# Recurrence stage: the key and query products of 64-row heads, split into two groups around a level's second half

## The reference

```
def step(state, inp):
    r_t, w_t, k_t, v_t, a_t, b_t = inp
    sa = jnp.einsum('bhvk,bhk->bhv', state, a_t)
    state = (state * w_t[:, :, None, :]
             + sa[..., None] * b_t[:, :, None, :]
             + v_t[..., None] * k_t[:, :, None, :])
    y_t = jnp.einsum('bhvk,bhk->bhv', state, r_t)
    return state, y_t
```

## Time and profile before

| | |
|---|---|
| median of three runs | 3224.02 us |
| the profiled execution's own time | 3229.49 us |
| its span, first to last instruction | 3227.9 us |
| mean granted TensorE clock | 0.985 |
| recurrence stage, first L2508 to last gate | about 970 to 1256 us of the span |
| one turn | about 34.8 us |

### The profile page before, as it was taken

One profiled execution on the slowest core, in us unless ns is written; L12 is line 12 of the kernel. 1 busy time (PEld: TensorE's weight loads), 2 busy tenths in 40 slices (PEclk: granted clock), 3 DMA queues, 4 the chain that ended last, 5 costly groups with the idle time before them and its releaser, 6 DMA issues.

```text
span 3227.9 us, 65591 instructions
## 1 busy us (share of the span) xinstructions
PE 3116.5 (97%) x23394; PEld 2702.9 (84%) x23394; DVE 2223.6 (69%) x3345; ACT 1524.2 (47%) x2171; POOL 368.2 (11%) x546
## 2 busy tenths in 40 slices
PE   7999999999999999999999999999999999999998
PEld 6887877877888888888888888888888888888887
DVE  6658766588866775775767667776667757666675
ACT  5543444567546765443434334443444434344443
POOL 2001032100124541100000000100012000000002
PEclk9999999989999999999999999999999999999999
DMA  6555555456761113666666666677446666666664
GB/s 199 161 159 135 142 163 164 143 160 181 207 193 50 36 39 86 182 189 187 183 188 188 184 183 186 173 184 193 132 121 183 183 188 184 186 183 187 187 185 144
DMA packets 1001331, 524.53 MB, mean 163 GB/s; under 512 B 25734, under 2 KB 996380, under 8 KB 1000668
## 3 DMA queue, kind: packets, MB, share of 16 engines
q1 hardware_dynamic: 995756, 507.99, 56.2%
q0 software_dynamic: 4608, 13.31, 1.2%
q10 hardware_dynamic: 816, 1.11, 0.1%
HBM read 513.95 MB, written 8.39 MB: 162 GB/s over the span
## 4 chain that ended last, share of the span: by engine, by line
PE 86%; DVE 6%; ACT 3%; issue 3%; POOL 1%; DMA 0%; ACTq 0%; DVEq 0%; POOLq 0%; SPq 0%
PE proj L305 50%; PE proj L307 25%; DVE w_low L260 1%; PE side L2391 1%; ACT w_high L273 1%; DVE g L317 1%; PE side L2508 1%; DVE w_low L276 1%; ACT w_high L254 1%; PE side L2549 0%; PE side L2372 0%; PE side L549 0%; DVE g L2818 0%; DVE g L2822 0%; PE side L2423 0%
## 5 line engine op out<-in xcount | busy, mean ns | idle before, releaser
L305 PE MATMUL proj<-b_pair,w_high 128*128 128x512 f32 x3872 | 1377.0, 400 | 24.3 <-DVE b_pair L1128 9.9
L305 PE MATMUL proj<-a_pair,w_high 128*128 128x512 f32 x3664 | 1297.7, 399 | 36.9 <-DVE a_pair L1801 10.2
L276 DVE TENSOR_TENSOR w_low<-w_raw,w_high 128x1024 fp32r<-128x1024 f32 x688 | 838.3, 1225 | 407.4 <-ACT w_high L273 402.7
L307 PE MATMUL proj<-b_pair,w_low 128*128 128x256 f32 x3872 | 1086.2, 281 | 0.0
L307 PE MATMUL proj<-a_pair,w_low 128*128 128x256 f32 x3664 | 1029.0, 281 | 0.0
L273 ACT ACTIVATE w_high<-w_raw 128x1024 fp32r<-128x1024 f32 x696 | 732.4, 1058 | 533.8 <-PE proj L307 529.6
L305 PEld LDWEIGHTS proj<-b_pair,w_high 128*128 128x128 f32 x3872 | 731.3, 189 | 203.4 <-issue 11.7
L305 PEld LDWEIGHTS proj<-a_pair,w_high 128*128 128x128 f32 x3664 | 691.5, 189 | 207.2 <-issue 19.8
L307 PEld LDWEIGHTS proj<-b_pair,w_low 128*128 128x128 f32 x3872 | 734.4, 190 | 0.2
L307 PEld LDWEIGHTS proj<-a_pair,w_low 128*128 128x128 f32 x3664 | 695.6, 190 | 0.1
L260 DVE TENSOR_TENSOR w_low<-w_raw,w_high 128x1024 fp32r<-128x1024 f32 x276 | 354.1, 1291 | 220.5 <-ACT w_high L254 214.3
(11 more groups left out here) (593 smaller groups left out, 2568.0 us busy)
## 6 DMA issues: line engine op xcount, KB each, us to landing
w_raw<-in_mlp_w_up_dram SPq DMA_DIRECT2D x256, 512.0 KB, 4.3
w_raw<-in_mlp_w_down_dram SPq DMA_DIRECT2D x256, 512.0 KB, 4.0
w_raw<-in_w_in_dram SPq DMA_DIRECT2D x112, 512.0 KB, 4.0
w_raw<-in_rwkv_w_rkv_dram SPq DMA_DIRECT2D x96, 512.0 KB, 4.3
w_raw<-in_w_kvf_dram SPq DMA_DIRECT2D x64, 512.0 KB, 4.1
w_raw<-in_w_out_dram SPq DMA_DIRECT2D x32, 512.0 KB, 4.1
w_raw<-in_rwkv_w_o_dram SPq DMA_DIRECT2D x32, 512.0 KB, 4.0
w_raw<-in_fox_w_q_dram SPq DMA_DIRECT2D x32, 512.0 KB, 4.2
```

The source lines that it names most:

```text
L276: eng.tensor_tensor(wl[slot][:], raw[slot][:], wh[slot][:].bitcast(F32), ALU.subtract)\
L305: pe.matmul(ps[bank][:, :].rearrange("p (a n) -> p a n", a=2), wh[slot][:, k, :], pair[:, :, kk, :], start=kk == 0, stop=False)
L307: mm = pe.matmul(ps[bank][:, 0:S], wl[slot][:, k, :], pair[:, 0, kk, :], start=False, stop=kk == KT - 1)
```

## The change

Each product of a level becomes a product over one head's own 64 partitions, with 128 moving columns, and `products` is called twice. The first call, between the halves of the level as before, does head 0 of set 0 and head 1 of set 1, for both chunks; it makes all the waits of both sets first, and raises a new semaphore `rw_first_heads` after its last matmul. The second call, behind the second half of the level and ahead of `spreads` or the gate, waits for that semaphore, does head 1 of set 0 and head 0 of set 1, and raises `rw_part` for set 0 and set 1. Neighbouring matmuls of a call lie in different halves of the partitions and in different PSUM banks. Nothing is changed on the other engines.

```diff
-            def products(i, left, right):
-                for s in range(2):
-                    d = RW_S[s]
-                    pe.wait_ge(sem("rw_kt"), pv(i, s))
-                    if right == "at":
-                        if i < LAST:
-                            pe.wait_ge(sem("rw_sig"), pv(i + 1, s))
-                    else:
-                        pe.wait_ge(sem("rw_rt"), pv(i, s))
-                        pe.wait_ge(sem("rw_taken"), part(i, s, "AK" if left == "bt" else "RB"))
-                    for c in range(2):
-                        mm = pe.matmul(quads(3 * s + 2)[:, :, c, :], d[left][:, P * c:P * c + P], d[right][i % 2][:, :, P * c:P * c + P],
-                                       start=True, stop=True)
-                    mm.then_inc(sem("rw_part"), 1)
+            def products(i, left, right, crossed):
+                nth = 3 * i + (0 if right == "at" else 1 if left == "bt" else 2)
+                if crossed:
+                    pe.wait_ge(sem("rw_first_heads"), nth + 1)
+                else:
+                    for s in range(2):
+                        pe.wait_ge(sem("rw_kt"), pv(i, s))
+                        if right == "at":
+                            if i < LAST:
+                                pe.wait_ge(sem("rw_sig"), pv(i + 1, s))
+                        else:
+                            pe.wait_ge(sem("rw_rt"), pv(i, s))
+                            pe.wait_ge(sem("rw_taken"), part(i, s, "AK" if left == "bt" else "RB"))
+                for c in range(2):
+                    for s in range(2):
+                        h = s ^ crossed
+                        d = RW_S[s]
+                        mm = pe.matmul(quads(3 * s + 2)[:, h, c, :], d[left][rng(h), P * c:P * c + P],
+                                       d[right][i % 2][rng(h), h, P * c:P * c + P], start=True, stop=True)
+                        if crossed and c:
+                            mm.then_inc(sem("rw_part"), 1)
+                if not crossed:
+                    mm.then_inc(sem("rw_first_heads"), 1)
...
+            CROSSED = {1: ("kt", "at"), 2: ("bt", "rt"), 3: ("kt", "rt")}
...
-                        products(i, "kt", "at")
+                        products(i, "kt", "at", 0)
                     elif lv == 2:
-                        products(i, "bt", "rt")
+                        products(i, "bt", "rt", 0)
                     elif lv == 3:
-                        products(i, "kt", "rt")
+                        products(i, "kt", "rt", 0)
...
                         mm.then_inc(sem("rw_g"), 1)
+                    if lv in CROSSED:
+                        products(i, *CROSSED[lv], 1)
                     if lv == 1 and i:
                         spreads(fin)
```

## The result

The changed kernel takes 3253.3 us, the median of five runs (3244.8 to 3258.2), against 3227.5 us for the kernel before (five runs): a ratio of 1.0081, 95% interval 1.0065 to 1.0097. The change costs some 26 us.

What follows compares the result with a forecast made beforehand. TensorE and ScalarE were both taken as full in levels 1 to 4, ScalarE with about 1 us of slack. Round trip 12 + clock 15 = +27 us on 3229.5, less 5.5 to the runs' median: 3251 us, range 3226 to 3284.

Steps and rivals of the forecast that it cites:

- the round trip: Levels 1 to 3: ScalarE's L2200 copies wait for the second half, behind L2549, which waits for L2254; +12 us.
- the clock: TensorE's granted clock falls once a turn after the new waits; 2.2 us for each of seven turns, +15 us.
- The walk: Levels 1 to 4 of turn i = 3, step by step: delays +0.65, +1.6, +3.0, +2.0 us; 2.0 us a turn.
- the price of a half: Each product call on TensorE: 0.45 us with tiles side by side, plus 0.10 us for the tile shape.
- Turns 0 and 7 as 0: Outer turns of the recurrence: round-trip effect taken as 0, kept at -4 to +2 us.
- The prediction's own sign: A turn of 36.9 us at clock 1.00 would mean the price of the clock was the error.
- the middle of my bounds: Price of one clock fall: between 1.1 us (L2549 and second half) and 3.2 us (through level 4), taken as 2.2.
- The rival with the clock up: Round trip on ScalarE without clock falls: +12 us, 3236 us, no change; chance 0.26.
- the one with more falls: Clock falls twice a turn or stays down into the next level: +57 us, 3281 us; chance 0.13.
- TensorE alone: Levels 1 to 3: TensorE alone decides, saving 24 x 0.86 = 20.7 us, time 3203 us; chance 0.09.
- Halves not side by side: The 64-row tiles do not run side by side: +8 us over the forecast, 3259 us; chance 0.14.
- The rule on emptying PSUM: Tiling speeds up TensorE but not PSUM emptying, which may become the bound; by it time stays at 3224 us.

Runs made afterwards that it cites:

- the filled kernel: Changed kernel with dummy matmuls in TensorE's new waits, 4 at level 2 and 7 at level 3: 3248.0 us, ratio 1.0062.
- the padded kernel: Changed kernel with 32 tiny matmuls (128 instructions, half a fetch) once in the first turn's level 2: 3268.7 us, ratio 1.0132.
- both ahead, padded: Changed kernel with both product calls ahead of the level's second half, plus 32 tiny matmuls in turn 0: 3238.1 us, ratio 1.0040.
- reordered, shifted: Changed kernel, ScalarE and GpSimd reordered, with 128 pad instructions: placed ahead of the stage 3226.2 us, in turn 0 3229.8 us.
- the reordered kernel before: Kernel before, with ScalarE's takes and GpSimd's masks moved behind work that does not depend on them: 3224.0 us, ratio 0.9998.
- the new order: ScalarE's takes and GpSimd's masks moved behind independent work: on the changed kernel 3234.2 us (1.0018), on the kernel before 3224.0 us (0.9998).
- the kernel with twice as many products: Kernel before, each 128-row product matmul issued as two of 128 moving columns, in the old place: 3226.6 us, ratio 1.0006.
- the reordered padded kernel: Changed kernel, ScalarE and GpSimd reordered, with 32 tiny matmuls in turn 0: 3229.8 us, ratio 1.0009.
- the padded kernel before: Kernel before, with 32 tiny matmuls (128 instructions) in the first turn's level 2: 3227.2 us, ratio 1.0002.

## Why the prediction was right, and where its sum was not

The time (3251 forecast, 3253 measured) and the mechanism came out as forecast: TensorE waits for L2254, ScalarE for the second half's signal, and turns are longer again where the clock is low. The sum had two terms, 12 for the round trip and 15 for the clock; the runs give some 19.5 and 6. One is 7.5 too small, the other 9 too large, so that the total came within 2 us is luck. A third term, TensorE's stops for instructions, was not in the sum at all; it is part of the 19.5.

- **The round trip.** The walk had 2.8 us from L2254's start to the end of L2200; turn 5 has 2.87 at level 2 (1177.52 to 1179.30 + 1.09) and 2.82 at level 3. Against level 1's L2254, the table load L2180 behind level 1's copies comes 1.03 us later than in the earlier trace rows (forecast 0.65), L2185 behind level 2's copies 2.03 (1.6), level 4's L2254 3.26 (3.0), and L2563 2.48 (2.0, against the earlier trace rows). All of these are 0.3 to 0.5 above the forecast, from level 1 on, so the error lies there. (The prediction's signs call these two loads those of levels 2 and 3.) **The step that failed is the price of a half, at level 1 above all**: I took 0.45 + 0.10 us for the first half and a start 0.04 after the gates. It took 0.68 (1171.57 to 1172.25) and started 0.14 after (1170.59 + 0.84); the second half's first signal came 0.74 after its start (1172.94 to 1173.68) instead of 0.64. In the halves of this turn the next two steps from pair to pair took 0.11 us, as assumed, but the first took 0.18 to 0.22, and in this half the last as well.
- **Turns 0 and 7 as 0.** Also wrong: with the waits filled they are 2.8 and 1.0 us longer than before, while turns 1 to 6 are 15.7 longer together (225.9 against 210.2). That makes 19.5 instead of 12. Turns of 37.3 against 34.9 us explain 6 x 2.4 = 14.4 of this; the 1.3 left are the two turns with stops, 2.1 us longer still, less 0.8 by which the turns before exceed 34.9 together. Turn 7 of the filled kernel has three stops of 2.2 us in all, so its 1.0 need not be the round trip's; why turn 0 is longer is open.
- **The clock.** This term was mis-sized most: 7 falls of 2.2 us against 6 us in all. The prediction's own sign for it came true: turns 4 and 5 are long, 37.5 and 37.3 us for its 36.9, at a clock of 1.00. There was not one fall a turn: turns 4 and 5 had none, turn 3 two short ones. And a fall costs less than the middle of my bounds: two falls, 10.2 us at 1.2 GHz together, cost 3.5 us a turn in the padded kernel, a third of their length. (That this is so little because only part of a turn's path is TensorE's is argued.) The rival with the clock up describes turns 4 and 5 and the filled kernel, though that takes 3248 us and not its 3236; the one with more falls describes the padded one. The executions of the changed kernel lie between: over their 13 us of spread the granted clock goes from 0.980 to 0.975.
- **TensorE alone.** Its 20.7 us are not there. Where the round trip and the stops are away, a turn is 34.9 us (both ahead, padded) or 34.0 (reordered, shifted), against 34.5 in the reordered kernel before. The first of these shows what is late next; TensorE's timeline in its turn 4, and VectorE's beside it:

```profile
1148.82 0.98 PE L2517 MATMUL side<-g 32*32 32x32 f32 x64 [0.65 <-DVE g L2596]
```

```profile
1146.85 0.93 DVE L2682 SCALAR_TENSOR_TENSOR g<-g,prm 128x256 f32<-128x256 f32 x1 [1.15 <-POOL g L2093]
1147.70 0.85 DVE L2682 SCALAR_TENSOR_TENSOR a_scratch<-a_scratch,prm 128x256 f32<-128x256 f32 x1
1148.48 0.28 DVE L2596 COPY_PREDICATED g<-m_blk,side 128x128 f32<-128x128 uint8 x1
```

  TensorE is early and waits for VectorE's masked copy, which stands behind the weighted keys (the line of the earlier trace rows), which wait for GpSimd. The saving itself is smaller too: the two halves take 0.68 + 0.64 = 1.32 us at level 1 against 1.82, 0.5 instead of 0.7. (Without the extra change of shape the prediction's own figures make 0.82 a level, not 0.86, and 19.7 us in all.)
- **Halves not side by side.** Excluded by the pairs above. The factor is 1.4 (1.82 to 1.32), not 2: each half has its slow first step and 0.20 us to the next shape.
- **The rule on emptying PSUM.** The rule of the Trainium skill that the prediction cites (TensorEngine Tiling (Array Packing), section PSUM Bottleneck) says that tiling does not speed up the emptying of PSUM, and TensorE's saving did not come through. But the emptying held nothing up in the old kernel, where the new order is worth nothing in time; it did in the changed one, where the order is worth 19 us. The rule does not say that the change makes the same copies later; that was the loss.
- **Slips without weight.** In level 3 of the walk TensorE would be done with the first half near 92.3 by the rows, not 92.5, and stand 2.4 us; measured were 2.06. The end of the last record is 0.25, not 0.27.

## What to carry to other kernels

When a producer's signal is moved, walk the consumer's queue, not the producer's. Here 0.5 us less work on TensorE put one round trip into each of three levels on an engine that had 1 us of slack, and the repair was on that engine's queue: put work that does not depend on the signal ahead of the wait. And an edit that packs TensorE's work into dense runs of short matmuls may expose it to instruction fetches; shift the code by half a fetch before believing, or blaming, a result of less than a per cent.

## What the runs showed of the hardware that was not expected

TensorE can run out of instructions. All 83 stops stand at the same place in the count of its records by 256, each 2.15 to 3.16 us behind the start of a fetch. A fetch brings about 253 recorded instructions, and TensorE's runs of 64 small matmuls use 128 in 0.69 us (L2559 above, 1172.25 to 1172.94), so one fetch feeds about 1.4 us of such code. Most fetches pass without a stop of 0.3 us all the same: the fourteen kernels make 787 of them from 965 to 1285 us. In the kernel before 1.7 us with only 16 instructions, the old products, lay between two such runs. That this is what kept it free of most stops (0.8 us in all) is argued from these numbers and fits the kernel with twice as many products, but was not tried by itself. The Trainium skill, Runtime: NRT & Kernel Launch, section Instruction fetch mechanics, has fetches in blocks of 256 instructions and the cost of a block's end mostly hidden. The size agrees with the count above, and mostly hidden it is over all kernels, with 83 stops on 787 fetches; where the code is dense the trace does not agree, with 16 stops on 57 fetches, 13.4 us in one stage.

Padding code with tiny matmuls may not be free either. Thirty-two of them took 2.2 to 3.6 us on TensorE in turn 0. In the profile of the reordered padded kernel the granted clock fell 1.0 us after the pad's start and stood at 0.5 for 30.7 us, and that turn took 47.8 instead of 35.3 us; in the changed padded kernel it stood there for 30.7 us from the pad's end on, in the padded kernel before for 6.8 us, against 3.4 without the pad. What makes it stay low so long is open.
